# Expert output weighted on eviction and added into one DRAM table, in place of a row store with two gathers per token

## What is computed

```python
# hier_moe: each token has one group and two experts of it, each with a weight
out = jnp.zeros_like(t)
for e in range(N_EXPERTS):                                   # 16 experts
    he = jax.nn.silu(t @ w_gate[e]) * (t @ w_up[e])          # 1024 -> 512
    out = out + dense_w[:, e:e + 1] * (he @ w_down[e])       # 512 -> 1024
# encoder_layer and trunk
x = x + g2 * out
y = rms_norm(x, final_norm_g)
```

## Time and profile before

| | |
|---|---|
| Median of three runs | 897.73 us (895.46 to 900.43) |
| Profiled execution | 894.43 us, of which 892.6 us are the span from first to last instruction |
| TensorE busy in the span | 773.3 us, 87% |
| VectorE, ScalarE, GpSimd busy | 60%, 44%, 26% |
| Expert part, from the first gather to the last down product | 541.6 to 855.6 us |
| From there to the end of the span | 37.0 us, TensorE idle |
| TensorE clock granted in the span | 0.921 of full speed on average, 1.00 from 580 to 831 us |

### The profile page before, as it was taken

The page is one execution under the profiler, slowest core; times in us unless marked ns, Lnnn a source line. Parts: engine busy times, 40 slices in busy tenths (PEclk is TensorE's granted clock), DMA queues, the critical chain, the costliest instruction groups (busy, mean ns, idle before and its releaser), DMA issues.

```text
span 892.6 us, 10120 instructions
## 1 busy us (share of the span) xinstructions
PE 773.3 (87%) x3811; PEld 615.6 (69%) x3811; DVE 537.4 (60%) x670; ACT 391.6 (44%) x454; POOL 232.0 (26%) x123
## 2 busy tenths in 40 slices
PE   4598999969999999988799755899999999999920
PEld 2376777747788888767578734788888877888710
DVE  1355544340446454496703666788888888888827
ACT  1442222312324334242321423677677776777514
POOL 0253333323122232224923102123222332220030
PEclk9599999989799999999999666999999999999975
DMA  9787565537112121142310872799999999997343
GB/s 329 254 241 233 163 180 177 172 129 218 47 48 72 48 64 51 52 151 75 94 48 1 350 332 72 262 379 411 385 396 390 407 400 378 386 394 280 117 173 157
DMA packets 74976, 189.99 MB, mean 213 GB/s; under 512 B 12946, under 2 KB 43770, under 8 KB 68796
## 3 DMA queue, kind: packets, MB, share of 16 engines
q1 hardware_dynamic: 66336, 160.51, 49.8%
q0 software_dynamic: 4848, 17.59, 5.7%
q10 hardware_dynamic: 3756, 11.41, 3.2%
HBM read 172.71 MB, written 16.78 MB: 212 GB/s over the span
## 4 chain that ended last, share of the span: by engine, by line
PE 54%; DVE 22%; issue 13%; ACT 4%; DMA 4%; ACTq 1%; POOL 0%; SPq 0%; POOLq 0%; DVEq 0%
PE psum L666 39%; DVE moe_low L1905 11%; ACT half_high L1287 2%; DMA xbuf<-x_sample 2%; PE psum L719 2%; PE psum L737 2%; PE psum L896 2%; PE psum L834 1%; PE psum L658 1%; PE psum L876 1%; PE psum L759 1%; DVE slot L1518 1%; PE psum L855 1%; PE psum L846 1%; DVE xsT_low L1914 1%
## 5 line engine op out<-in xcount | busy, mean ns | idle before, releaser
L2020 POOL TENSOR_TENSOR low_ring<-front_ring,high_ring 128x1024 fp32r<-128x1024 f32 x54 | 131.4, 2435 | 320.5 <-ACT high_ring L1116 320.5
L1116 ACT ACTIVATE high_ring<-front_ring 128x1024 fp32r<-128x1024 f32 x54 | 57.1, 1058 | 233.7 <-PE psum L666 201.1
L666 PE MATMUL psum<-h_low,high_ring 128*128 128x512 f32 x312 | 118.2, 396 | 0.0
L666 PE MATMUL psum<-h_high,high_ring 128*128 128x512 f32 x312 | 116.9, 391 | 0.0
L666 PE MATMUL psum<-h_high,low_ring 128*128 128x512 f32 x280 | 114.4, 408 | 1.1 <-POOL h_low L2028 0.5
L1905 DVE TENSOR_TENSOR moe_low<-front_ring,half_high 128x2048 fp32r<-128x2048 f32 x48 | 107.9, 2285 | 10.3 <-ACT half_high L1287 10.3
L666 PE MATMUL psum<-half_high,xsT_low 128*128 128x512 f32 x256 | 103.2, 403 | 10.4 <-DVE xsT_low L1914 6.3
L666 PE MATMUL psum<-moe_low,xsT_high 128*128 128x512 f32 x256 | 101.2, 395 | 0.0
L666 PE MATMUL psum<-half_high,xsT_high 128*128 128x512 f32 x256 | 101.1, 395 | 0.0
L1287 ACT ACTIVATE half_high<-front_ring 128x2048 fp32r<-128x2048 f32 x48 | 91.1, 1915 | 8.4 <-PE psum L666 8.4
L1905 DVE TENSOR_TENSOR moe_low<-slots,half_high 128x2048 fp32r<-128x2048 f32 x32 | 73.1, 2286 | 13.1 <-ACT half_high L1287 13.1
(11 more groups left out here) (269 smaller groups left out, 1325.7 us busy)
## 6 DMA issues: line engine op xcount, KB each, us to landing
front_ring<-w_down SPq DMA_DIRECT2D x16, 2048.0 KB, 11.4
front_ring<-w_in SPq DMA_DIRECT2D x34, 512.0 KB, 5.3
xbuf<-ada_w SPq DMA_DIRECT2D x32, 512.0 KB, 4.2
slot<-w_gate SPq DMA_DIRECT2D x8, 2048.0 KB, 10.1
slots<-w_up SPq DMA_DIRECT2D x8, 2048.0 KB, 9.9
slots<-w_gate SPq DMA_DIRECT2D x8, 2048.0 KB, 10.1
front_ring<-w_up SPq DMA_DIRECT2D x8, 2048.0 KB, 9.8
y_rows<-inout ACTq DMA_DIRECT2D x16, 512.0 KB, 11.2
```

Source lines behind the costliest of these rows:

```text
L666: mm = pe.matmul(out, lhs(a, k), rhs(b, k), start=(start and k == 0 and a == 1), stop=(stop and k == count - 1 and (a, b) == (0, 0)))
L1116: act.activation(dst, src.rearrange("p (k n) -> p k n", k=KD), ACT.Copy).then_inc(high_ready, 1)
L2020: pool.tensor_tensor(low, src, high.bitcast(F32), ALU.subtract).then_inc(low_ready, 1)
```

## The change

- The eviction of the down product is ScalarE's alone: both banks in one instruction of 1024 columns, scaled by the weight of each slot (`w_now`, one column per buffer). VectorE's `last_row` is gone.
- ScalarE issues no store any more. GpSimd has a new step `add_rows` for each tile: it waits for the eviction, copies the tile's column of `ids` as destinations, and issues an indirect DMA that adds the 128 rows of `ybuf` to the rows of a DRAM table `y_sum` of 512 rows. It then waits on its own queue until that DMA has landed, and copies the weights of the tile after next to `w_now`. It has to wait, since two tiles can add to the same token.
- An empty slot now has id 1024, which is out of bounds (the last row is 511), so the gather and the add leave it out. The gather buffers are zeroed once, at about 500 us.
- The weights in slot order (`slot_w`) come from a further product of one-hot matrices, just behind `ids` (eight more instructions on VectorE and on TensorE, and a copy).
- After the last add SyncE loads the four tiles of `y_sum`. VectorE multiplies by g2, adds the residual and normalises. The output stores are split between ScalarE (tiles 0 and 2) and SyncE (1 and 3). The table `pos`, the eight gathers, the scaling by ScalarE and the scale-and-add of VectorE are gone.
- The early store of zeros fills the 512 rows of `y_sum` in place of 1024 rows of `y_rows`. The table of the square root is loaded before the last normalisation begins.

The core of the diff:

```diff
-                                 .to_broadcast([P, 2 * (MAX_PAIRS - MIN_PAIRS), D])).then_inc(zeros_stored, 16)
+                                 .to_broadcast([P, TT, D])).then_inc(zeros_stored, 16)
...
+            wait_added(sp, 0, last_pair + 1)
+            wait_added(sp, 1, last_pair + 1)
+            for t in range(TT):
+                sp.dma_start(y_sums[t], y_sum[t * P:(t + 1) * P, :]).then_inc(sums_landed[t], 16)
+            for t in (1, 3):
+                sp.wait_ge(y_ready, t + 1)
+                sp.dma_start(y_out[t // TPR][0, t % TPR * P:(t % TPR + 1) * P, :], xbuf[:, t, :]
+                             ).then_inc(out_stored, 16)
...
+            name = "slot_w"
+            wait_bank(pe, name)
+            pe.wait_ge(hot_weights_ready, 2 * TT)
+            product(name, bank(name, 2 * MAX_PAIRS), lambda n: hot_place[n], lambda n: hot_weight[n], 2 * TT)
...
                 if before:
-                    pe.wait_ge(y_act, s + -1)
-                    pe.wait_ge(y_dve, s + -1)
+                    pe.wait_ge(y_act, s)
...
                 act.wait_ge(half_used, half_count(s, DOWN, 1) + 1)
+                act.wait_ge(w_ready, s)
                 if stored is not None:
-                    act.wait_ge(y_stored[q], stored * 16)
-                act.activation(ybuf[:, q, 0:COLS], psum[:, 5, :], ACT.Copy).then_inc(y_act, 1)
-                act.wait_ge(y_act, s)
-                act.wait_ge(y_dve, s)
-                act.dma_start(y_rows[bass.ds((s + -1) * P, P), :], ybuf[:, q, :]).then_inc(y_stored[q], 16)
-
+                    wait_added(act, q, stored)
+                act.activation(ybuf[:, q, :], psum[:, 5:7, :].rearrange("p b n -> p (b n)"), ACT.Copy,
+                               scale=w_now[:, q:q + 1]).then_inc(y_act, 1)
...
-                a, b = pair[2 * t], pair[2 * t + 1]
-                dve.wait_ge(first_ready, t + 1)
-                dve.wait_ge(pair_landed[2 * t + 1], 16)
-                link(dve.scalar_tensor_tensor(out=a, in0=b, scalar=topw[:, t, 1:2], in1=a, op0=ALU.mult, op1=ALU.add))
+                a = y_sums[t]
+                dve.wait_ge(sums_landed[t], 16)
                 link(dve.tensor_tensor(a, a, g2b[:, t // TPR, :], ALU.mult))
...
+            def add_rows(m, q, stored, weights=True):
+                pool.wait_ge(y_act, m + 2)
+                pool.tensor_copy(dest_now[:, q:q + 1], ids[:, bass.ds(m, 1)])
+                pool.drain()
+                pool.indirect_dma_start(y_sum, bass.IndirectOffsetOnAxis(ap=dest_now[:, q:q + 1], axis=0),
+                                        ybuf[:, q, :], None, bounds_check=TOK - 1, oob_is_err=False,
+                                        compute_op=ALU.add).then_inc(y_stored[q], 16)
+                wait_added(pool, q, stored)
+                if weights:
+                    pool.tensor_copy(w_now[:, q:q + 1], slot_w[:, bass.ds(m + 2, 1)]).then_inc(w_ready, 1)
...
+            with pool.Fori(2, last_pair) as i:
+                fetch(i * 2 + 2, 0)
+                add_rows(i * 2 + -2, 0, i)
+                fetch(i * 2 + 3, 1)
+                add_rows(i * 2 + -1, 1, i)
+            add_rows(last_pair * 2 + -2, 0, last_pair)
+            add_rows(last_pair * 2 + -1, 1, last_pair)
+            add_rows(last_pair * 2, 0, last_pair + 1, False)
+            add_rows(last_pair * 2 + 1, 1, last_pair + 1, False)
```

More of the change, by code:

```diff
@@ L199, in list_groups @@
     g += [("rank", "v")] + [(f"spread{b}.{r}", "s") for b in range(10, 12) for r in range(REQS)]
-    g += [("ids", "v")]
+    g += [("ids", "v"), ("slot_w", "v")]
     return g
@@ L351, in hybrid_layer @@
         sqjunk = hTf[:, 0:1024]
-        pair = ([mqkf[:, n * D:(n + 1) * D] for n in range(4)]
-                + [slot3[:, n * D:(n + 1) * D] for n in range(4)])
+        y_sums = [slot3[:, n * D:(n + 1) * D] for n in range(TT)]
         ids = placed_over("ids", "mvb", 0, [P, 2 * MAX_PAIRS], U32)
-        pos = sb("pos", [P, TT, 2], U32)
         topw = mvf[:, 32:40].rearrange("p (t n) -> p t n", n=2)
@@ L363, in hybrid_layer @@
         hot_tile = [route[:, 256 + n * 24:280 + n * 24] for n in range(2 * TT)]
+        hot_weight = [route[:, 448 + n * 24:472 + n * 24] for n in range(2 * TT)]
+        slot_w = mvf[:, 64:64 + 2 * MAX_PAIRS]
+        w_now = mvf[:, 96:98]
+        dest_now = placed_over("dest_now", "mvb", 104, [P, 2], U32)
         moe_slot = [slot3[:, :], slots45[:, 0, :], front_ring[:, 1, :], slots45[:, 1, :],
@@ L429, in hybrid_layer @@
         zeros_stored = sem("zeros_stored")
-        rows_stored = sem("rows_stored")
+        xs_cleared = sem("xs_cleared")
+        hot_weights_ready = sem("hot_weights_ready")
+        w_ready = sem("w_ready")
+        sums_landed = [sem(f"sums_landed{i}") for i in range(TT)]
         xs_landed = [sem(f"xs_landed{i}") for i in range(2)]
@@ L1897, in _ @@
             wait_full(dve, "ids")
-            emptied(dve.tensor_copy(ids[:, :], bank("ids", 2 * MAX_PAIRS)))
+            emptied(dve.tensor_scalar(ids[:, :], bank("ids", 2 * MAX_PAIRS), float(2 * TOK), None, ALU.add))
+            for t in range(TT):
+                for n in range(2):
+                    dve.tensor_scalar(hot_weight[2 * t + n], lc["iota"][:, 0:2 * MAX_PAIRS], tile_of[:, t, n:n + 1],
+                                      topw[:, t, n:n + 1], ALU.is_equal, ALU.mult).then_inc(hot_weights_ready, 1)
             def low_half(n, place, slot, h):
@@ L1927, in split_he @@
                                   heT[0].bitcast(F32), ALU.subtract).then_inc(heT_ready, 1)
[L1929 to L1935, removed]
             low_half(0, 0, GATE, 0)
+            wait_full(dve, "slot_w")
+            emptied(dve.tensor_copy(slot_w[:, :], bank("slot_w", 2 * MAX_PAIRS)))
             low_half(1, 1, GATE, 1)
@@ L1947, in _, with tile_step @@
             split_he(0)
-            def tile_step(s, q, stored, last=False):
+            def tile_step(s, q, last=False):
                 low_of_tile(s, q, UP, 1)
@@ L1965, in tile_step @@
                         low_half(last_pair * 12 + (10 + h), 2 + h, 5, h)
[L1966 removed]
                 split_he(s)
             last_pair = load_last_pair(dve)
[L1970 to L1973, removed]
[L1974 to L1980 removed]
+            tile_step(1, 1)
+            tile_step(2, 0)
+            with dve.Fori(2, last_pair + 1) as i:
+                tile_step(i * 2 + -1, 1)
+                tile_step(i * 2, 0)
+            tile_step(last_pair * 2 + 1, 1, last=True)
             def normalise_row(t):
@@ L2069, in _ @@
             gather(1, ids[:, 1:2])
+            wait_emptied(pool, "slot_w")
+            for m in range(2):
+                pool.tensor_copy(w_now[:, m:m + 1], slot_w[:, m:m + 1]).then_inc(w_ready, 1)
             def fetch(s, q):
```

78 lines of the change are left out of this document (29 added, 49 removed).

## The result

The changed kernel takes 912.73 us (median of 4 runs, 906.11 to 913.9), the kernel before 897.5 us beside it: 1.015 times as long, 95% interval 1.010 to 1.021. The forecast was 889, faster; what came is the size and sign of the first rival, 918 us. The profiled execution took 913.9 us, its span 911.8.

A forecast was written before the change was run, and what follows sets the result against it. TensorE was taken to set the pace of the tiles. Start -1.3, rounds -1.5, GpSimd's queue 0 and tail -5.6 gave -8.4 us: 886.0 for the profiled execution, 889.4 at the median, range of 8 in 10 from 884 to 920.

The forecast's parts named there:

- first rival: GpSimd's queue bounds the rounds because adds read two places and land in 13.5 us: 918 us, chance 0.25.
- start, ids to the first hidden rows: First gather's issue on GpSimd, no longer slowed by VectorE's splits: -1.3 us, between 0 and -2.5.
- rounds, behind the start: The tiles' rounds lose VectorE's copy and ScalarE's wait, both mostly hidden beside TensorE: -1.5 us, between 0 and -1.8.
- GpSimd's queue: Waiting for each add's landing on GpSimd makes its queue lag slightly, at no cost to TensorE: 0 us.
- tail, from the last eviction: Last eviction to the end, with fewer VectorE instructions and stores split over queues: -5.6 us.
- Between copy and issue stand 0.83 us: On GpSimd, the gap from copying row numbers to issuing an add, taken from a fetch: 0.83 us.
- fetch and copies: GpSimd's work per round: a fetch of 5.86 us and two copies of 1.2 us each.
- L: Time from an add's issue on GpSimd to its landing, taken as 10 us.
- decides from L = 11.1: The landing time above which GpSimd's lag would make TensorE wait and the first rival hold: 11.1 us.
- third rival: Empty slots, though left out of the result, still cost their place in transfers: 930 us or more, chance 0.05.
- Waits cost 0.14 us a round: In the tiles' rounds TensorE sets the pace: 18.69 us mostly, 18.55 without waits, so 0.14 us a round recoverable.
- second rival: In the tail, the last add takes 13.5 us even without weights beside it: 897 us, no change, chance 0.10.

The follow-up runs named there:

- e5: Changed kernel with semaphores for drains in GpSimd's loop, weights copied ahead of the add, landing awaited only before the next add: 883.37 us, 0.985 of before.
- e1: Changed kernel with the drain between the add's copy of row numbers and its issue replaced by a semaphore: 890.42 us, 0.990 of before.
- e2: Kernel before with one more drain on GpSimd behind each gather of the loop, where nothing waits for it: 898.41 us, 1.001 of before.
- e9: As e5, but with the old drain back in the fetch, behind an add in flight: 887.77 us, 0.990 of before.
- e7: Kernel before with ScalarE's wait for VectorE's half and the store moved behind the eviction of the hidden rows: 891.58 us, 0.993 of before.
- e4: Kernel before with ScalarE alone evicting both halves of the down product, unweighted, all else as it was: 889.87 us, 0.990 of before.
- e8: As e5, but the rows are written into the sum instead of added: 878.52 us, 0.979 of before.

## Why the prediction was wrong

The terms of the sum, in the profiled executions (us; e5 shows them with the queue out of the way):

| term | predicted | after | e5 |
|---|---|---|---|
| start, ids to the first hidden rows | -1.3 | -0.2 | -0.4 |
| rounds, behind the start | -1.5 | +21.2 (all) | -7.3 |
| of the rounds and tail: GpSimd's queue | 0 | about +31 | 0 |
| tail, from the last eviction | -5.6 | -3.8 | -6.0 |

The queue's row is after less e5: 28.7 us up to the last eviction and 2.2 behind it.

**GpSimd's queue: the step that failed.** "Between copy and issue stand 0.83 us" gave the add the same 0.83 us, and it took 8.2. That row is a fetch with nothing in flight ahead of its drain; an add stands behind the gather just issued, and its drain lasts until that gather has landed. No row read for the prediction shows such a drain. (The 1.77 us at 549.42 us in the same group, with the first two gathers issued 5 to 8 us ahead, look like one; but in e1 the same place holds 1.83 us, though the copy there starts at 551.33 us and the second gather, issued at 545.82, landed 5.4 us later.) The budget's other figures erred the other way: fetch and copies were put at 8.26 us and were 3.1, since GpSimd's copies mostly came when VectorE was itself waiting. L was put at 10 from the issue and measured 10.3 in the median, 11.1 in the mean with the handover, just the limit that the prediction gave. So the round was 3.1 + 8.2 + 11.1 = 22.4 us against 8.26 + 0.83 + 10 = 19.1, and the missing term alone carries it past the point of harm. e1 and e2 show this; e9 shows it for the add. Taking the drain out, e1 gave back 20 of the 31 us (18.0 up to the last eviction, 2.1 behind it). The other 10.7 us, 317.9 against e5's 307.2, go with what e5 moves, above all the wait for the landing, and are a second error in the same term: with the gather in flight beside it L is 13.1 us, 14.8 in the mean with the handover, and not 10, so a queue that waits out each landing is late even without the drain.

**The first rival** had the right consequence and place, and a cause that holds for the smaller part. Its signs came nearly as written: rounds mostly over 20 us from the fifth on, ScalarE's eviction behind GpSimd, and TensorE behind both that and the late gathers. That its size came out too, 918 us for 912.7 and a round of 22.6 us for 22.4, is luck: it has no drain, and its price rested on L = 13.5 with 8.26 us of fetch and copies. In the changed kernel L was 10.3, and most of the loss was the drain's; in e1, without that drain, L is 13.1, and its mechanism is what is left, 10.7 us. In e5 L is 13.5 and costs nothing. Its "decides from L = 11.1" held only for a queue that waits out each landing before it goes on, and that was an arrangement, not a fact of the chip.

**The third rival** is out. GpSimd's DMA queue (packets, MB, share of the engines) moved 17.59 MB before, and now:

```profile
q0 software_dynamic: 6000, 13.40, 5.4%
```

The 4.19 MB less are 1024 rows of 4 KB, the number of empty slots in the gathers; the adds of 1024 filled rows took the place of the eight gathers behind the loop, 1024 rows too.

**The rounds were mis-sized, and the reading at fault is the chain.** "Waits cost 0.14 us a round" took the one round of the earlier trace rows, at 755 us, for the pattern; it lay just behind the stretch in which the chain runs elsewhere. The chain of the kernel before ahead of it (start, length, what):

```profile
717.27 2.20 DVE moe_low L1905
719.47 0.61 DVE inout L1935
...
720.30 0.34 ACTq L1314
720.64 0.05 issue
720.69 0.05 ACT heT_high L1302
...
721.19 1.92 ACT half_high L1287
723.13 0.05 DVE moe_low L1905
```

VectorE's eviction releases ScalarE's store, behind it come the hidden rows and the next split of weights, and that releases VectorE: a loop of the two engines beside TensorE, on the chain from 600 to 750 us. ScalarE's idle time for VectorE's half, which the prediction called nearly all hidden, was part of it: with that wait moved, e7 gained 3.8 us. A round could fall from 18.69 us to TensorE's own 17.95, not to 18.55. The prediction's own rows said so: the earlier trace rows leaves TensorE 0.98 us idle in 37.00, 0.49 us a round and not 0.14. And the 48 matmuls that the earlier trace rows shows as one piece, 11.25 us, take 10.99 in e4's chain (at 751.79 us), 0.26 us less; why the piece is longer there the trace doesn't show. Together that is the 0.75 us. The term was worth 7.0 us (e4), and the changed kernel's second to fourth rounds show it too, before the queue fell behind. With this term right and the queue at 0 the sum would have been 14 us below before, near what e5 gained, 12.5.

**The start** came out short. TensorE's first transposes stand 5.80 us behind the ids (542.72 to 548.52) and not 6.68, 0.9 of the 1.3 foreseen, but no gather holds them any more: the first lands 4.1 us behind its issue at 543.87 us (TensorE, idle time and releaser at the end):

```profile
544.67 3.58 PE L677 MATMUL psum<-mvb,rot_pT 128*128 128x24 f32 x16 [1.99 <-DVE mvb L1908]
548.52 1.97 PE L1004 MATMUL psum<-early,inout 128*128 128x128 f32 x8 [0.28 <-DVE mvb L1942]
```

The product for `slot_w`, 3.58 us, and VectorE's copy of it now stand ahead of them; the prediction costed that product on VectorE and left TensorE's part out. By the first hidden rows only 0.2 us are left. Most of what went is TensorE's clock, which the prediction had left out here: it is granted at 0.50 (1.2 GHz) from 553 to 557 us, for the first 4.0 us of multiplying, where before it was so for 2.7 (551.66 to 554.36); ahead of that TensorE had been busy for 5.30 of 8.00 us (545 to 553) and, before, for 1.95 of 8.60.

**The tail** was right in size: -6.0 in e5, where the way from the last eviction to the product with g2 is 11.6 us (849.68 to 861.32), predicted 12.2. (Three times 1.28 us is 3.8 and not 3.9, a slip without effect.) In the changed kernel the last adds stand behind one another:

```profile
878.59 1.11 ACT L1395 ACTIVATE inout<-psum,mvb 128x1024 f32<-128x1024 f32 x1 [6.73 <-PE psum L685]
...
881.87 0.18 POOL L2089 COPY dest_now<-ids 128x1 uint32 x1 [4.82 <-DMA y_sum<-inout,dest_now]
882.93 1.57 POOL L2091 DMA_INDIRECT y_sum<-inout,dest_now  x1 [0.88 <-issue]
...
892.41 1.23 DVE L1993 TENSOR_TENSOR slot<-slot,og 128x1024 f32<-128x1024 f32 x1 [19.82 <-DMA slot<-y_sum]
```

The last tile's rows are ready at 879.70 us, and GpSimd comes to them at 881.87, when the add ahead has landed: the 2.2 us. VectorE's chain is 15.5 us from there (892.41 to 907.88), as predicted, and the end follows 3.9 us behind, 3.7 predicted. The second rival, a late last add, did not come: alone it lands in 6.0 us, 6.1 taken. That two adds stand one behind the other, which spoke for it, cost those 2.2 us.

## What to carry to other kernels

Where two transfers share an engine's queue, look at what stands between their issues: a drain there can put their landings in series, and it costs nothing in a trace until something stands behind it. Wait for a landing where its result is used, not where it was issued. Here drain and early wait together cost 29 us (after against e5); writing in place of adding gained 17 us with both in place and 5 without them. Follow the chain of waits through the whole stage before calling one engine its bound; a single round without waits may be the exception.

## What the runs showed of the hardware

- A drain on GpSimd waits for gathers (14.0 us in e2) and for adds (12.8 in e9) issued ahead of it, and takes 0.33 us in the median with nothing in flight (in the changed kernel; 2.2 in e2, where the copy ahead of it took 2.1); a semaphore counted by the copy did the same service in 0.8 us from copy to issue, with a gather in flight (e1).
- Adding rows to DRAM lands in 6.0 us alone (e5) where writing them takes 3.2 (e8), 1.9 times. The Trainium skill's rule in Collectives: The Full Stack, section "The bandwidth ceiling: the fold count and why AG ≠ RS ≠ AR", of half the rate because two sources are read, fits these two; they don't test it, since a landing holds more than the moving of bytes (the issue alone takes 1.6 us for an add and 1.0 for a write). Beside the loads of weights it was 13.5 for 10.9, 1.24 times, and there the rule doesn't show.
- Gathers that leave out the empty slots, half of all, moved half the bytes. With the DMA engines full (share 0.99) they landed in 8.8 us in the median between writes (e8) and 12.6 between adds (e5); full tiles took 13.5. The shortest landing stayed at 4.1 us (e5); how full that tile was isn't shown.
